# Storing the last output from SyncE, one store per token tile and half, in place of GpSimd

## The reference, cut to what matters

```
for l in range(2):
    x = layer_norm(ALPHA*x + 0.5*swiglu(x, wg[l,0], wu[l,0], wd[l,0]), ln_g[l,0], ln_b[l,0])
    y, new_state = token_mixing(x, ...)        # three kinds of heads, reads caches, gives new cache rows
    x = layer_norm(ALPHA*x + y, ln_g[l,1], ln_b[l,1])
    x = layer_norm(ALPHA*x + 0.5*swiglu(x, wg[l,1], wu[l,1], wd[l,1]), ln_g[l,2], ln_b[l,2])
return y_prompt (1,256,1024), y_sample (8,1,1024), and twelve arrays of new cache rows and states
```

## Time and profile before

| | us |
|---|---|
| median of 3 runs | 1436.84 (1436.48 to 1442.02) |
| the profiled execution, its time | 1435.87 |
| its span, from the first to the last instruction | 1434.1 |
| PE busy in it | 1321.0 (92%) |
| POOL busy in it | 118.4 (8%) |
| the last stretch in which the page's chain of waits names PE | ends at 1418.82 |
| the last counted instruction (a store's issue on POOL) | ends at 1421.16 |

### The profile page before, as it was taken

One profiled execution on the slowest core, in us unless ns is written; L12 is line 12 of the kernel. 1 busy time (PEld: TensorE's weight loads), 2 busy tenths in 40 slices (PEclk: granted clock), 3 DMA queues, 4 the chain that ended last, 5 costly groups with the idle time before them and its releaser, 6 DMA issues.

```text
span 1434.1 us, 24304 instructions
## 1 busy us (share of the span) xinstructions
PE 1321.0 (92%) x9753; PEld 1163.5 (81%) x9753; DVE 802.1 (56%) x1483; ACT 520.5 (36%) x762; POOL 118.4 (8%) x207
## 2 busy tenths in 40 slices
PE   5999997999998989999799999799899987999993
PEld 4999996656775789999799999766477666999992
DVE  5555546774665265554565544577547545555433
ACT  3333335410453263333353333334025434333321
POOL 9000002012000010000200000200120001000001
PEclk9999998997899989999989999899969998999996
DMA  8555577447164336646735546764632631565540
GB/s 260 180 181 167 148 209 256 144 147 244 46 176 119 93 110 185 190 132 162 217 121 178 175 132 173 237 240 133 206 127 73 163 117 60 177 187 167 155 108 30
DMA packets 251909, 226.81 MB, mean 158 GB/s; under 512 B 11716, under 2 KB 234066, under 8 KB 249634
## 3 DMA queue, kind: packets, MB, share of 16 engines
q1 hardware_dynamic: 245282, 204.08, 48.1%
q0 software_dynamic: 6528, 21.37, 4.3%
HBM read 221.55 MB, written 3.86 MB: 157 GB/s over the span
## 4 chain that ended last, share of the span: by engine, by line
PE 84%; DVE 9%; ACT 3%; issue 2%; DMA 1%; SPq 1%; POOL 0%; DVEq 0%
PE bank L746 21%; PE bank L747 21%; PE bank L748 21%; PE bank L665 9%; PE bank L855 3%; PE bank L1012 2%; PE bank L755 1%; PE bank L933 1%; PE bank L756 1%; PE bank L883 1%; PE bank L835 1%; DVE bc_pages L1656 1%; ACT x L1227 1%; DVE rstd L1755 1%; DVE w_low L1510 1%
## 5 line engine op out<-in xcount | busy, mean ns | idle before, releaser
L746 PE MATMUL bank<-x_high,w_low 128*128 128x264 f32 x1408 | 406.1, 288 | 27.6 <-DVE x_low L1492 23.3
L747 PE MATMUL bank<-x_low,w_high 128*128 128x264 f32 x1408 | 403.1, 286 | 0.0
L748 PE MATMUL bank<-x_high,w_high 128*128 128x264 f32 x1408 | 402.6, 286 | 0.0
L1510 DVE TENSOR_TENSOR w_low<-weights,w_high 128x2048 fp32r<-128x2048 f32 (+1 forms) x172 | 347.7, 2039 | 69.5 <-ACT w_high L1206 55.9
L746 PEld LDWEIGHTS bank<-x_high,w_low 128*128 128x128 f32 x1408 | 268.8, 191 | 31.6 <-issue 27.9
L747 PEld LDWEIGHTS bank<-x_low,w_high 128*128 128x128 f32 x1408 | 269.8, 192 | 0.0
L748 PEld LDWEIGHTS bank<-x_high,w_high 128*128 128x128 f32 x1408 | 268.3, 191 | 0.0
L746 PE MATMUL bank<-hidden_high,w_low 128*128 128x264 f32 x704 | 205.0, 291 | 0.0
L748 PE MATMUL bank<-hidden_high,w_high 128*128 128x264 f32 x704 | 199.8, 284 | 0.0
L747 PE MATMUL bank<-hidden_low,w_high 128*128 128x264 f32 x704 | 199.2, 283 | 0.0
L1248 ACT ACTIVATE w_high<-weights 128x2048 fp32r<-128x2048 f32 (+1 forms) x88 | 163.9, 1862 | 8.2 <-DMA weights<-in_ffn_wu_dram 8.2
(11 more groups left out here) (302 smaller groups left out, 1686.8 us busy)
## 6 DMA issues: line engine op xcount, KB each, us to landing
weights<-in_ffn_wg_dram SPq DMA_DIRECT2D x44, 1024.0 KB, 5.5
weights<-in_ffn_wu_dram SPq DMA_DIRECT2D x44, 1024.0 KB, 8.0
weights<-in_ffn_wd_dram SPq DMA_DIRECT2D x64, 704.0 KB, 6.3
weights<-in_w_in_dram SPq DMA_DIRECT2D x20, 1024.0 KB, 5.5
bc_pages<-in_cache_bc_kv_dram SPq DMA_DIRECT2D x128, 128.0 KB, 2.1
weights<-in_w_out_dram SPq DMA_DIRECT2D x16, 512.0 KB, 8.3
weights<-in_cache_bw_kv_dram SPq DMA_DIRECT2D x16, 256.0 KB, 3.3
ring<-in_cache_bw_kv_dram SPq DMA_DIRECT2D x16, 256.0 KB, 3.2
```

The costliest lines, as they stand in the source:

```text
L746: mm(out, w_low, v_high, start=start, stop=False)
L747: mm(out, w_high, v_low, start=False, stop=False)
L748: return mm(out, w_high, v_high, start=False, stop=stop)
L1510: tt(low(k, half), raw(k, half), high(k, half).bitcast(F32), ALU.subtract).then_inc(low_done, 1)
```

## The change

The six stores of the final output move from the end of POOL's stream to the end of SP's. There were four stores: per half one of both prompt tiles and one of the samples. There are now six: per half one for each prompt tile, issued as soon as that tile's copy has raised `stage_ready` (at 1, 2, 4 and 5), and one for the samples (at 3 and 6). The bytes are the same. The wait for `y_stored` moves to SP as well; six stores raise it to 96. POOL still waits for `rows_stored` and `states_stored`.

```diff
@@ block.sync, behind the last ffn(l, 1, WOUT_USE + 2)
+            for half in range(2):
+                col = slice(half * 512, (half + 1) * 512)
+                for t in range(TT):
+                    sp.wait_ge(stage_ready, 3 * half + t + 1)
+                    sp.dma_start(y_prompt[0, t * P:(t + 1) * P, col], stage[:, t, col]).then_inc(y_stored, 16)
+                sp.wait_ge(stage_ready, 3 * (half + 1))
+                sp.dma_start(y_sample.rearrange("b s d -> (b s) d")[:, col], stage[0:DEC, TT, col]).then_inc(y_stored, 16)
+            sp.wait_ge(y_stored, 16 * 6)
@@ block.gpsimd, at its end
-            for half in range(2):
-                col = slice(half * 512, (half + 1) * 512)
-                pool.wait_ge(stage_ready, 3 * (half + 1))
-                pool.dma_start(y_prompt[0].rearrange("(t p) d -> p t d", p=P)[:, :, col], stage[:, 0:TT, col]).then_inc(y_stored, 16)
-                pool.dma_start(y_sample.rearrange("b s d -> (b s) d")[:, col], stage[0:DEC, TT, col]).then_inc(y_stored, 16)
             pool.wait_ge(rows_stored, 16 * 8 * DEPTH)
             pool.wait_ge(states_stored, 16 * 4 * DEPTH)
-            pool.wait_ge(y_stored, 64)
```

## The result

The changed kernel has a median of 1422.70 us in 4 runs (1421.46 to 1423.49), the kernel before 1438.39 (1436.48 to 1442.02) beside it: a ratio of 0.9889, with a 95% interval of 0.9869 to 0.9909. The forecast was 1425.0, in a range from 1422.5 to 1431.0. The direction and the cause were right, and the gain is larger than forecast. The profiled execution took 1422.40, its span is 1420.6. Before, these were 1435.87 and 1434.1; as before, 1.8 us lie outside the span.

What follows compares the result with a forecast made beforehand. The end was taken to be bound by POOL's late DRAIN. 1419.59 + 0.1 + 2.4 + 0.25 + 0.12 + 0.2 = 1422.7 span, 1424.5 profiled, 1425 median; range 1422.5 to 1431.

Steps and rivals of the forecast that it cites:

- the sum: The path from the last copy's semaphore at 1419.59 to the span's end, forecast at 1422.7 against 1434.1, 11.4 us less.
- the landing: From the start of SP's last store issue until that store has landed, forecast at 2.4 us, between 2.1 and 2.7.
- the tail: From the start of DVE's last copy to the span's end, 15.25 us before; 11.4 us less forecast.
- What bounds the end: After PE's last matmul, POOL's DRAIN of 10277 ns, starting late because POOL first waits for the final output's stores.
- POOL's DRAIN takes its full price early, off the path: After POOL's last subtractions, the DRAIN starts near 1410.4, takes 10.28 us again and ends at 1420.7, before the stores do.
- The cover: Time between POOL's DRAIN ending at 1420.7 and SP's signal arriving at 1422.5: 1.8 us to spare.
- The stores on SP: Six issues at SP's end, 0.33 us each, none waiting for the one before; the last starts after 0.1 us.
- The end on SP: From SP's released wait to the span's end: 0.25 us to the DRAIN, 0.12 for it, 0.2 for semaphores and release.
- the step from the profile to the median: Median of runs taken as 1.0 us above the profiled execution, turning 1424.5 into 1425.4.
- The range: Forecast median between 1422.5 and 1431 us, to hold 8 in 10, with two tenths of a per cent for scatter.
- The DRAIN stays last: Rival at the program's end: a 10 us DRAIN still follows the last stores; gain only 1.3 us, chance 0.13.
- SP's issues become slow: Rival at SP's final stores: each issue costs 4.3 us, making the kernel 9.4 us slower; chance 0.03.

Runs made afterwards that it cites:

- the three measurements of kernels with this tail: The changed kernel (0.9889), the same once more with nothing edited (0.9933), and the changed kernel with POOL's DRAIN left out (0.9941), each against the kernel before.

## Where the prediction was right, and which of its terms failed

The mechanism held, and the size failed. From 1436.84 the forecast gain was 11.8 us; by the ratio it was 15.9. The step of the sum that failed is the landing, put at 2.4 us with bounds of 2.1 and 2.7, and measured at 1.48. With the shorter end on SP it makes the tail's share of the miss, 12.6 us gained for 11.4 forecast. The other 3.3 us of the 15.9 aren't in the tail; the range put too little aside for scatter between runs to hold them.

**What bounds the end: right.** 10.28 of the idle 10.8 us at the earlier trace rows were POOL's DRAIN; without it the tail of the kernel before is 10.3 us shorter, with nothing else changed. Why the DRAIN takes 10 us the prediction left open; that it goes by the number of DMAs came out in the experiments.

**POOL's DRAIN takes its full price early, off the path: right,** and of the two ways that the prediction left open it was the one taken, for caution and not for a reason. Its start was read from the end of the subtractions, and the sequencer in fact came to it 3.7 us before their end. What counts is its end: forecast 1420.7, measured 1419.25. Of the 1.45 us, 0.87 is the earlier end of everything upstream in this execution, 0.33 the four DMAs fewer, and some 0.25 the way from a released wait to the DRAIN, which POOL didn't have to go. The cover was put at 1.8 us to spare; it was 1420.4 - 1419.25 = 1.15, since SP's end came sooner as well.

**The stores on SP: right.** 0.30 to 0.37 us an issue against 0.33 to 0.35; none waited for the one before; the last began 0.04 us behind its copy's semaphore, against 0.1.

**The landing: this is the term that was mis-sized.** Forecast 2.4 us, with 2.1 and 2.7 as its ends; measured 1.48, below both. The row taken for it, POOL's 16 KB stores of 2.7 us, stood right behind 512 KB in one store, and the end waits for both. The prediction noted that the fifth store is issued 0.9 us ahead, and didn't take the bytes off the price. The four combinations give it: on POOL 2.7 with four stores and 2.0 with six, on SP 2.6 and 1.48. So splitting is worth 0.7 to 1.1 of the landing, and SP 0.1 to 0.5. The 0.8 us that the prediction gave the bytes of the fifth store were taken from the earlier trace rows, and these show POOL's stores alone. Which of the last two stores landed last can't be told, as both raise one semaphore.

**The end on SP: right in kind, 0.2 too long.** Forecast 0.57 from the released wait to the span's end (0.25, 0.12 and 0.2), measured 0.38: 0.17 to the DRAIN, 7 ns for it and 0.2 for the rest. The earlier trace rows had SP's DRAIN right behind an issue, 123 ns; behind a long wait it took 7.

Together the tail from `stage_ready` on was forecast at 3.07 us and measured at 1.9: 1.2 us too long, 0.9 of it the landing. With 0.87 us upstream that is the 2.1 us by which the profiled time, 1422.40, lies below the 1424.5 of the sum. The rest is the step from the profile to the median: it was put at +1.0, as in the kernel before, and was +0.3.

**The range: its lower end was too near.** Two tenths of a per cent were allowed for scatter between runs. With the best bounds, 11.8 us less, that is 1436.84 - 11.8 - 2.9 = 1422.1, and not the 1423 of the prediction; even with the 12.6 us of the tail it is 1421.3, still above 1420.9. The tails give 12.6 us, a ratio of 0.9912 with all else equal; the three measurements of kernels with this tail gave 0.9889, 0.9933 and 0.9941. Two of their intervals miss 0.9912, one on each side, so the first ratio most likely overstates the change and the third understates it. The scatter lies upstream, in the same instructions, and moves medians by some us: those of the kernel before were 1434.62 to 1438.39, those of the changed kernel 1422.70 and 1426.85. The second ratio, 0.9933, would be 1427.2 from 1436.84, inside the range, so on which side of its lower end a comparison fell was in part chance. What causes the scatter stays open.

**The rivals.** *The DRAIN stays last* fell: SP's DRAIN took 7 ns right behind the last landing, and POOL's ended before it. Its forecast, a gain of 1.3 us, is near the 1.2 us that the issuer alone gave while POOL's end was still last. That is where the rule of the Trainium skill has its place ("DMA: Bandwidth & Descriptors", section "Issuing engines are not separate DMA queues"): for a swap of the issuer alone the runs agree that little is saved. In the changed kernel the measurement decides, and it is 12.6. *SP's issues become slow* fell with 0.30 to 0.37 us an issue.

## What to carry to other kernels

Look at the last instructions of every engine's stream and at the sequencers' rows behind them: this program ended when its last engine had run its DRAIN, and a DRAIN that no busy share counts was 10 us of 1434. GpSimd, when it has issued many DMAs, should reach its end early, or run a DRAIN where it has time, and leave the last wait to an engine whose DRAIN is short, here SP. The cover is worth counting: here 1.15 us were to spare, some 14 DMAs on GpSimd at 82 ns (an estimate from these rows), before POOL's DRAIN would be last again.

## What the runs showed of the hardware

Behind DMAs that had landed, GpSimd's DRAIN took 0.04 us and 0.082 us for each DMA that GpSimd had issued since its last DRAIN, whether they had landed just before or long ago, and whether other work lay between (118 and 119 ns for one load; 1359 for 16, 5269 for 64; 9950, 10277 and 10440 for 121, 125 and 127). Gathers, loads and stores counted alike within what these sums can tell (0.03 us of 10). Right behind eight stores, some still under way, two DRAINs took longer, 9.6 and 8.0 us after 93 and 28 DMAs, where the count gives 7.6 and 2.3; right behind four stores and after 125 DMAs in all one took 10.28, which is the count. Why they differ stays open. SP, with hundreds of DMAs behind it, had DRAINs of 7 to 204 ns.

POOL's sequencer entered a DRAIN while its engine still worked, so the DRAIN's duration in the trace contains that work (13.65 us for 9.98 of its own); the end of the row is what can be relied on.
